# Moving the modulation weight rows: other places in SyncE's load queue, and one block in VectorE's order

## The chip, the cores and the metric

The kernel runs on one core of a Trainium2 chip. The metric is device microseconds of one launch. Three executions of the kernel before took 957.76, 957.87 and 953.32 us, so the median is 957.76 us.

## The reference, cut to what matters

Everything is float32, for one sequence of 256 tokens with 1024 features. A first model (an mLSTM layer, a feed-forward stage, a softmax attention, a second feed-forward stage) is followed by a second model of two layers. Each of these two layers is modulated by a conditioning vector, and the change is about that vector's weights:

```python
c_act = jax.nn.silu(c)                       # 1024 numbers
for l in range(DEPTH):                       # two layers
    mod = c_act @ w_ada[l] + b_ada[l]        # 3072 numbers
    shift, scale, gate = jnp.split(mod, 3, axis=-1)
    h = rmsnorm_2(x, g_pre[l]) * (1.0 + scale[:, None, :]) + shift[:, None, :]
    p = h @ w_in[l]
    ...                                      # convolution branch, attention branch
    x = x + gate[:, None, :] * rmsnorm_2(y, g_post[l])
```

`mod` depends only on `c` and on weights, so it can be computed at any time before layer `l` needs `shift`, `scale` and `gate`.

## The kernel before, in words

**The engines' shares.** TensorE (PE) does all matrix products, VectorE (DVE) and ScalarE (ACT) the elementwise work, GpSimd (POOL) sums of down-projection weights, and SyncE (SP) issues nearly all weight loads from one in-order queue. Every engine has its own fixed program; semaphores join them. Nothing is planned at run time: the order is the order of the code.

**The modulation product.** It is done on DVE. `w_ada` is stored transposed and cut into 48 tiles of 128 x 1024 (512 KB), 24 for each layer; this text calls them ada tiles 0 to 47. `load_ada(first, last)` (L416) issues their loads into `ada_w`, which holds three. For tile n from 3 on it first makes SP wait until DVE has used up tile n - 3. DVE's `ada(count)` (L2165) takes the next `count` tiles in turn: it waits for the tile's load and then multiplies by `c_row`, the silu of `c` broadcast to all partitions, with a sum along the row, one column of `mod`. `modulation(l)` (L2174) adds the bias, `layer_gains(l)` (L2186) forms the gains that layer `l` uses.

**Where DVE takes them.** Tiles 0 to 10 in the 11 steps of the first feed-forward stage, 11 to 14 in its down product, 15 to 20 one for each head in heads 1 to 6 of the first attention (L2453), 21 to 31 and 32 to 35 in the second feed-forward stage, and 36 to 47 in the tail of layer 0: two at L2654, four at L2661 (tiles 38 to 41), then the first half of the convolution branch is gated (`y2_conv`, L2671), two more (42, 43, L2668), the second half is gated, two (44, 45, L2674), and the last two (46, 47, L2708) inside the output norm of token half b = 0, whose end also holds `modulation(1)` and `layer_gains(1)`.

**Where SP loads them.** Among the loads of the ring and of the feed-forward weights. The ring has eight buffers for 64 weight blocks of 1 MB (two of 800 KB). `load(n)` first waits until the product that used the block's last holder is done. Block 51 goes to the buffer of block 43, which holds `w_pw2` of layer 0, so `load(51)` makes SP wait until PE has finished the pointwise product `feat(n + 11, ...)` of layer 0 (L1767 to L1769). `load_up` and `load_down` bring the feed-forward weights into `fring`; `ffn_loads(f)` (L424) holds most of them, with one ada tile for each step.

**PE around the change.** In layer 0 the tail is: pointwise product; wait for `y2_conv` 1; `mix(0, 0, 0, 2)`; wait for `y2_conv` 2; the other mixes; `turn_back(0)` and `turn_back(1)`, which need the norm's diagonals; then layer 1. In the first attention PE's head n needs DVE's scaled probabilities of the head before it, and DVE takes its ada tile after these:

```python
                    if between is not None:
                        between(n)        # ada(1) for n = 1 to 6
```

Of the kernel before, what the change touches and what calls it, by code (L numbers as in the profile page):

```python
# [22 lines left out]
P = 128  # L23
T = 256
TB = T // P
D = 1024
DC = D // P
# [7 lines left out]
DEPTH = 2  # L35
# [76 lines left out]
def model(nc, I, out):  # L112
    with ExitStack() as ctx:
# [5 lines left out]
        def S(name):  # L119

            if name not in sems:
                sems[name] = ctx.enter_context(nc.semaphore(name))
            return sems[name]
# [15 lines left out]
        rstd = sb("rstd", [P, 2 * T])  # L139
# [249 lines left out]
        def _(sp):  # L389
# [26 lines left out]
            def load_ada(first, last):  # L416

                for n in range(first, last):
                    if n >= 3:
                        sp.wait_ge(S("ada_free"), n - 2)  # L420
                    at = D * (n % 24)
                    sp.dma_start(ada_w[:, n % 3, :], I["ada"][n // 24][:, at:at + D]).then_inc(S(f"ada{n % 3}"), 16)

            def ffn_loads(f):  # L424

                a = (0, 21)[f]
                sp.wait_ge(S("up_done"), FF_STEPS * f + 1)
                load_up(f, 2, FF_STEPS * f % 2)
                for i in range(3, FF_STEPS):
                    load_up(f, i, (FF_STEPS * f + i) % 2)  # L430
                    load_down(f, 0, i - 1)
                    load_ada(a + i, a + i + 1)
                load_down(f, 1, 0)
                load_down(f, 1, 1)
                load_down(f, 0, FF_STEPS - 1)
                for i in range(2, FF_STEPS):
                    load_down(f, 1, i)
                    if 3 <= i < 6:
                        load_ada(a + 8 + i, a + 9 + i)
                    if i == 9:  # L440
                        load_ada(a + 14, a + 15)
                load_ada(a + 15, a + 18)

            for m, (k0, k1) in enumerate(FIRST):
# [10 lines left out]
            load_up(0, 0, 0, True)  # L455
            for n in range(8, 16):
                load(n)
            sp.dma_start(c_row[:, :], I["c_2"][0].partition_broadcast(P)).then_inc(S("row_in"), 16)
            load_ada(0, 3)
            product(sp, 11)  # L460
            load_up(0, 1, 1, True)
            for i in (0, 1):
                load_down(0, 0, i, True)
            for n in range(16, 20):
                load(n)
            sp.wait_ge(S("rows_out"), 16)
            row = 3 * P + 1
            sp.dma_start(bass.AP(skewed, 0, [[row, P], [P * row, 8], [1, 3 * P]]),
# [4 lines left out]
                load(n)  # L473
            product(sp, 25)
            sp.wait_ge(S("tok_out"), 20)
            load_ada(18, 21)
            for i in (0, 1):
                load_up(1, i, 1 - i)
                load_down(1, 0, i, True)
            load_ada(21, 24)  # L480
            for n in range(32, 36):
                load(n)
            ffn_loads(1)
# [4 lines left out]
            for l in range(DEPTH):  # L488
                if l > 0:
                    sp.wait_ge(S("vals_done"), 2 * l)  # L490
                sp.dma_start(w_qidx.rearrange("p k n -> p (k n)"), I["w_qidx"][l])\
                    .then_inc(S("small_in"), 16)
                sp.dma_start(w_uv_all, I["w_uv"][l]).then_inc(S("small_in"), 16)
                if l == 0:
                    sp.wait_ge(S("bias_skewed"), 16)
                    for dst, at, wide in ((biasT[:, :, 0:P], 2 * P - 1, P), (biasT[:, :, P:DIAG], P - 1, T)):
                        sp.dma_start(dst, bass.AP(skewed, at, [[3 * P, P], [P * row, 8], [1, wide]]))\
                            .then_inc(S("bias_in"), 16)
                    for n in range(40, 48):
                        load(n)  # L500
                else:
                    for n in range(48, 51):
                        load(n)
                    load_ada(39, 45)
                    load(51)
                    load_ada(45, 48)
                    for n in range(52, 64):
                        load(n)
            sp.wait_ge(S("gains_set"), 2)
# [1291 lines left out]
        def _(dve):  # L1801
# [665 lines left out]
            def layer(l):  # L2467
# [202 lines left out]
                    x = y2[:, 2 * m:2 * m + 2, :]  # L2670
                    v.tensor_tensor(x, x, three(pb[m][:, :], 2), ALU.mult).then_inc(S("y2_conv"), 1)  # L2671

                if l == 0:
                    ada(2)  # L2674

                def gained_out(b, j):

                    dve.wait_ge(S("out_sq"), 4 * l + 2 * b + j + 1)
# [3 lines left out]
                for b in range(TB):  # L2682
# [20 lines left out]
                    else:  # L2703
                        ins.then_inc(S("ms_done"), 1)
                        dve.wait_ge(S("ms_done"), 4 + 2 * l + b)
                        then(v.tensor_scalar(other, half, -0.5, None, ALU.mult))
                        if l == b == 0:
                            ada(2)  # L2708
                        if l == 1:
                            dve.wait_ge(S("row_in"), 32)  # L2710
                            gained_out(b, 0)
# [8 lines left out]
                    dve.wait_ge(S("rstd_done"), nn + 1)  # L2720
                    if l == 0:
                        v.tensor_scalar(diag[:, b, :], ident, y, None, ALU.mult).then_inc(S("diag_done"), 1)
                        if b == 0:
                            modulation(1)
                            layer_gains(1)
                            v.memset(rstd[:, T:T + 1], 1.0)
                            v.tensor_copy(xr[:, :, T:T + 1], mod[:, 1, 0:DC].unsqueeze(2))
                    else:
                        dve.wait_ge(S("gained_out"), 2 * b + 2)
                        dve.wait_ge(S("tokens_cp"), 4)  # L2730
                        for lo, hi in OUT_PARTS[b]:
                            x = h_tok[:, b, lo:hi]
                            v.scalar_tensor_tensor(x, b_ytok[:, b, lo:hi], y, x, ALU.mult, ALU.add)\
                                .then_inc(S("out_ready"), 1)
# [100 lines left out]
```

## Time and profile before

| | |
|---|---|
| median of three runs | 957.76 us |
| the profiled execution's own time | 957.76 us |
| its span | 955.9 us |
| PE busy | 940.4 us (98%) |
| DVE busy | 791.2 us (83%) |
| ACT busy | 278.2 us (29%) |
| POOL busy | 152.0 us (16%) |
| share of PE in the chain that ended last | 88% |
| data moved | 171.8 MB, mean 180 GB/s |

The span is the time from the first to the last instruction; the own time lies 1.86 us above it. Busy time is the time in which an engine had an instruction of its own at work, and PE's matmuls are pipelined, so their durations overlap. The chain that ended last is followed back from the last instruction, at each step to what released it. Times in the rows further down are us from the start of the span, and a bracket at the end of a row says how long the engine stood idle before it and what it was waiting for.

### The profile page before, as it was taken

To read this page: it belongs to the slowest core of one execution; us is meant where nothing else is said; L and a number is where in the kernel's file an instruction comes from. 1 tells how busy PE (TensorE), PEld (TensorE's weight loads), DVE (VectorE), ACT (ScalarE), POOL (GpSimd) and SP (SyncE) were. 2 spreads that over 40 slices of the span, in tenths; PEclk is the share of its full clock that TensorE was granted. 3 is DMA by queue.
4 is the path that set the end of the run, shared out by engine and by line. 5 is a ranking of instruction groups with operands and counts; after the bars stand their busy time and mean duration, and the time that the engine had idled before them with its cause. 6 is when DMAs were issued, how large, how long until landed. Compare 5 with 4: busy or idle time off the path is not lost.

```text
span 955.9 us, 16133 instructions
## 1 busy us (share of the span) xinstructions
PE 940.4 (98%) x6456; PEld 868.9 (91%) x6456; DVE 791.2 (83%) x1690; ACT 278.2 (29%) x622; POOL 152.0 (16%) x139
## 2 busy tenths in 40 slices
PE   9999999999999999999999999999999999999997
PEld 7888999999999998888999999999888878888876
DVE  3778889999999469778799999995699986899963
ACT  1033122221222112254221212221434453624561
POOL 0000210212236520003002131268000000000000
PEclk9999999999999899999999999999999999999999
DMA  8942455363644460558354646446933428442101
GB/s 301 411 184 108 177 190 219 147 261 142 255 156 161 144 268 1 207 213 328 123 198 156 257 146 258 147 164 221 348 133 123 166 88 275 179 136 101 51 1 45
DMA packets 36859, 171.80 MB, mean 180 GB/s; under 512 B 5032, under 2 KB 8880, under 8 KB 23344
## 3 DMA queue, kind: packets, MB, share of 16 engines
q1 hardware_dynamic: 35120, 167.72, 47.7%
q10 hardware_dynamic: 1664, 3.04, 0.9%
q8 instruction: 51, 0.84, 0.4%
q14 instruction: 24, 0.20, 0.1%
HBM read 169.69 MB, written 2.64 MB: 180 GB/s over the span
## 4 chain that ended last, share of the span: by engine, by line
PE 88%; DVE 7%; DMA 2%; issue 1%; ACT 1%; ACTq 0%; SPq 0%; DVEq 0%
PE bank L1376 24%; PE bank L1396 12%; PE bank L1061 9%; PE bank L1479 5%; PE bank L1690 4%; PE bank L1129 3%; PE bank L1594 3%; PE bank L1352 3%; PE bank L1676 3%; PE bank L1575 3%; PE bank L1322 3%; PE bank L1136 3%; DVE work L2245 1%; PE bank L1072 1%; PE bank L1519 1%; DMA ring<-in_ring 1%
## 5 line engine op out<-in xcount | busy, mean ns | idle before, releaser
L1396 PE MATMUL bank<-work,fring 128*128 128x128 f32 x1008 | 118.5, 279 | 3.2 <-DVE work L2264 3.2
L534 POOL TENSOR_TENSOR fring<-fring 128x256 f32<-128x256 f32 x44 | 38.8, 881 | 511.3 <-DMA fring<-in_down 511.3
L1396 PEld LDWEIGHTS bank<-work,fring 128*128 128x128 f32 x1008 | 116.8, 196 | 3.6 <-POOL fring L539 3.2
L2493 DVE SCALAR_TENSOR_TENSOR work<-work,cols 128x256 f32<-128x256 f32 x240 | 98.8, 478 | 1.0 <-ACT work L915 0.5
L1376 PE MATMUL bank<-sq,fring 128*128 128x128 f32 x640 | 84.5, 275 | 0.0
L2170 DVE SCALAR_TENSOR_TENSOR ada_w<-ada_w,c_row 128x1024 f32<-128x1024 f32 x48 | 61.6, 1295 | 27.0 <-DMA ada_w<-in_ada 27.0
L746 ACT ACTIVATE work<-work,cols 128x256 f32<-128x256 f32 x88 | 47.8, 592 | 118.3 <-DVE work L2235 103.7
L2245 DVE SCALAR_TENSOR_TENSOR work<-work,cols 128x256 f32<-128x256 f32 x176 | 78.4, 517 | 2.6 <-ACT work L746 2.6
L1376 PE MATMUL bank<-sq,ring 128*128 128x128 f32 x640 | 78.0, 275 | 0.0
L1376 PE MATMUL bank<-ring,fring 128*128 128x128 f32 x640 | 78.0, 275 | 0.0
L1376 PEld LDWEIGHTS bank<-sq,fring 128*128 128x128 f32 x640 | 77.9, 192 | 0.0
L1376 PEld LDWEIGHTS bank<-ring,fring 128*128 128x128 f32 x640 | 74.8, 192 | 0.1
L1376 PEld LDWEIGHTS bank<-sq,ring 128*128 128x128 f32 x640 | 74.7, 192 | 0.0
L536 POOL TENSOR_TENSOR fring<-fring 128x512 f32<-128x512 f32 x44 | 67.0, 1522 | 3.5
L1690 PE MATMUL bank<-ring,fring 128*128 128x256 f32 x256 | 58.0, 380 | 1.0 <-DVE fring L2671 1.0
L1690 PEld LDWEIGHTS bank<-ring,fring 128*128 128x128 f32 x256 | 48.2, 190 | 8.1 <-DVE fring L2671 1.4
L539 POOL TENSOR_TENSOR fring<-fring 128x256 f32<-128x256 f32 x44 | 46.2, 1050 | 3.4
L1061 PE MATMUL bank<-work,ring 128*128 128x256 f32 x192 | 42.4, 379 | 0.0
L1061 PE MATMUL bank<-xg,ring 128*128 128x256 f32 x192 | 42.3, 380 | 0.0
L1376 PE MATMUL bank<-ring 128*128 128x128 f32 x320 | 42.3, 275 | 0.0
L1061 PEld LDWEIGHTS bank<-xg,ring 128*128 128x128 f32 x192 | 36.3, 190 | 5.1
L1061 PEld LDWEIGHTS bank<-work,ring 128*128 128x128 f32 x192 | 36.3, 190 | 4.9
(416 smaller groups left out, 1771.8 us busy)
## 6 DMA issues: line engine op xcount, KB each, us to landing
ring<-in_ring SPq DMA_DIRECT2D x60, 1024.0 KB, 6.9
fring<-in_up SPq DMA_DIRECT2D x44, 1024.0 KB, 6.9
ada_w<-in_ada SPq DMA_DIRECT2D x48, 512.0 KB, 6.3
fring<-in_down SPq DMA_DIRECT2D x44, 512.0 KB, 4.8
ring<-in_ring SPq DMA_DIRECT2D x2, 800.0 KB, 6.7
bias_skewed<-bias_rows SPq DMA_DIRECT2D x1, 1536.0 KB, 12.7
consts<-in_consts ACTq DMA_DIRECT2D x1, 1128.0 KB, 15.3
ring<-in_ring SPq DMA_DIRECT2D x2, 512.0 KB, 4.8
```

The costliest lines, as they stand in the source:

```text
L534: nc.gpsimd.tensor_tensor(s1, glo, ghi, ALU.add).then_inc(S("down_step"), 1)
L536: nc.gpsimd.tensor_tensor(w[:, 1280:1792], w[:, 0:512], w[:, 256:768], ALU.subtract)\
L539: nc.gpsimd.tensor_tensor(s4, vhi, s2, ALU.subtract).then_inc(S("down_sums"), 1)
L746: nc.scalar.activation(f_t[v][:, c, :], f_u[:, v, c, 0:T], ACT.Identity, bias=col(f"f_conv_b{f}", n), scale=col(f"f_conv_w{f}", n)).then_i ...
L1061: last = mm(bank[:, T * c:T * (c + 1)], w[:, k, at + P * c:at + P * (c + 1)], x[:, k, :], start=(k == 0), stop=(k == nk - 1))
L1376: last = mm(bank[:, P * at:P * (at + 1)], w[:, k, P * c:P * (c + 1)], x[:, k, :], start=(k == 0), stop=(k == 3))
L1396: last = mm(bank[:, at + P * c:at + P * (c + 1)], w[:, P * c:P * (c + 1)], x, start=(i == 0 and at == 0 and c == 0), stop=(i == FF_STEPS - 1),
L1479: last = mm(places[n], x[:, k, :], w[:, k, :], start=(k == 0), stop=(k == 3))
L1690: last = mm(bank[:, 0:T] if apart else bank[:, T * m:T * (m + 1)], y2[:, k, P * b:P * (b + 1)], slot8(load)[:, k, :], start=(k == 4 and (m ...
L2170: v.scalar_tensor_tensor(x, x, 1.0, c_row[:, :], ALU.mult, ALU.mult, accum_out=mod[:, l, j:j + 1])\
L2245: return v.scalar_tensor_tensor(f_t[q][:, c, :], f_u[:, q, c, t:t + T], col(f"f_conv_w{f}", 44 * t + 22 * q + 2 * i + c), f_t[q][:, c, :], ...
L2493: marks[c] = link(v.scalar_tensor_tensor(b_y[:, c, :], b_a[:, c, tap:tap + T], col("conv_w_2", 124 * l + 4 * tap + c), b_y[:, c, :], ALU.m ...
```

## The change

It changes only orders, in five places. In `ffn_loads` ada tile 14 (and tile 35 in the second stage) is loaded after the down tile of i = 6 and no longer after that of i = 9. The loads of `c_row` and of tiles 0 to 2 move from ahead of the wait for product 11 to behind the loads of ring blocks 16 to 19. Tiles 18 to 20 move from ahead of six feed-forward loads to behind them. Ring block 51 is loaded ahead of tiles 39 to 44 and no longer behind them. On DVE, in layer 0, the last two tiles, `modulation(1)`, `layer_gains(1)` and two small writes move out of the output norm's loop to just ahead of it. No tile changes the place in the order of tiles, and no computation is added or dropped.

```diff
--- before.py
+++ after.py
@@ -435,10 +435,8 @@
                 load_down(f, 0, FF_STEPS - 1)
                 for i in range(2, FF_STEPS):
                     load_down(f, 1, i)
-                    if 3 <= i < 6:
+                    if 3 <= i < 7:
                         load_ada(a + 8 + i, a + 9 + i)
-                    if i == 9:
-                        load_ada(a + 14, a + 15)
                 load_ada(a + 15, a + 18)
 
             for m, (k0, k1) in enumerate(FIRST):
@@ -455,14 +453,14 @@
             load_up(0, 0, 0, True)
             for n in range(8, 16):
                 load(n)
-            sp.dma_start(c_row[:, :], I["c_2"][0].partition_broadcast(P)).then_inc(S("row_in"), 16)
-            load_ada(0, 3)
             product(sp, 11)
             load_up(0, 1, 1, True)
             for i in (0, 1):
                 load_down(0, 0, i, True)
             for n in range(16, 20):
                 load(n)
+            sp.dma_start(c_row[:, :], I["c_2"][0].partition_broadcast(P)).then_inc(S("row_in"), 16)
+            load_ada(0, 3)
             sp.wait_ge(S("rows_out"), 16)
             row = 3 * P + 1
             sp.dma_start(bass.AP(skewed, 0, [[row, P], [P * row, 8], [1, 3 * P]]),
@@ -473,11 +471,10 @@
                 load(n)
             product(sp, 25)
             sp.wait_ge(S("tok_out"), 20)
-            load_ada(18, 21)
             for i in (0, 1):
                 load_up(1, i, 1 - i)
                 load_down(1, 0, i, True)
-            load_ada(21, 24)
+            load_ada(18, 24)
             for n in range(32, 36):
                 load(n)
             ffn_loads(1)
@@ -499,11 +496,9 @@
                     for n in range(40, 48):
                         load(n)
                 else:
-                    for n in range(48, 51):
+                    for n in range(48, 52):
                         load(n)
-                    load_ada(39, 45)
-                    load(51)
-                    load_ada(45, 48)
+                    load_ada(39, 48)
                     for n in range(52, 64):
                         load(n)
             sp.wait_ge(S("gains_set"), 2)
@@ -2670,9 +2665,13 @@
                     x = y2[:, 2 * m:2 * m + 2, :]
                     v.tensor_tensor(x, x, three(pb[m][:, :], 2), ALU.mult).then_inc(S("y2_conv"), 1)
 
-                if l == 0:
+                if l + 1 < DEPTH:
                     ada(2)
-
+                    ada(2)
+                    modulation(1)
+                    layer_gains(1)
+                    v.memset(rstd[:, T:T + 1], 1.0)
+                    v.tensor_copy(xr[:, :, T:T + 1], mod[:, l + 1, 0:DC].unsqueeze(2))
                 def gained_out(b, j):
 
                     dve.wait_ge(S("out_sq"), 4 * l + 2 * b + j + 1)
@@ -2704,8 +2703,6 @@
                         ins.then_inc(S("ms_done"), 1)
                         dve.wait_ge(S("ms_done"), 4 + 2 * l + b)
                         then(v.tensor_scalar(other, half, -0.5, None, ALU.mult))
-                        if l == b == 0:
-                            ada(2)
                         if l == 1:
                             dve.wait_ge(S("row_in"), 32)
                             gained_out(b, 0)
@@ -2720,11 +2717,6 @@
                     dve.wait_ge(S("rstd_done"), nn + 1)
                     if l == 0:
                         v.tensor_scalar(diag[:, b, :], ident, y, None, ALU.mult).then_inc(S("diag_done"), 1)
-                        if b == 0:
-                            modulation(1)
-                            layer_gains(1)
-                            v.memset(rstd[:, T:T + 1], 1.0)
-                            v.tensor_copy(xr[:, :, T:T + 1], mod[:, 1, 0:DC].unsqueeze(2))
                     else:
                         dve.wait_ge(S("gained_out"), 2 * b + 2)
                         dve.wait_ge(S("tokens_cp"), 4)
```

## Rows read from the trace of the kernel before

**Rows 1.** Page, part 1: busy us of each engine, share of the span, instructions
```profile
PE 940.4 (98%) x6456; PEld 868.9 (91%) x6456; DVE 791.2 (83%) x1690; ACT 278.2 (29%) x622; POOL 152.0 (16%) x139
```

**Rows 2.** Waits of PE: who was waited for, us in total, times, longest
```profile
PE bank L1396 <- DVE work L2264: 3.2, 2, 3.0
```

**Rows 3.** Timeline, SyncE's queue, layer 0's tail: start, us, instructions
```profile
782.28 12.28 SPq L422 DMA_DIRECT2D ada_w<-in_ada  x6
795.71 0.33 SPq L394 DMA_DIRECT2D ring<-in_ring  x1
796.08 3.74 SPq L422 DMA_DIRECT2D ada_w<-in_ada  x3
```

**Rows 4.** Timeline, PE and DVE, layer 0's tail
```profile
788.61 7.07 PE L1061 MATMUL bank<-work,ring 128*128 128x256 f32 x32
...
792.97 1.22 DVE L2170 SCALAR_TENSOR_TENSOR ada_w<-ada_w,c_row 128x1024 f32<-128x1024 f32 x1 [1.83 <-DMA ada_w<-in_ada]
...
794.12 0.68 DVE L2671 TENSOR_TENSOR fring<-fring,bank 128x512 f32<-128x512 f32 x1
...
795.52 1.89 PE L1690 MATMUL bank<-ring,fring 128*128 128x256 f32 x8
...
798.37 12.35 PE L1690 MATMUL bank<-ring,fring 128*128 128x256 f32 x56 [0.97 <-DVE fring L2671]
...
805.09 0.15 DVE L2686 TENSOR_SCALAR sml<-sml 128x1 f32<-128x1 f32 x1
```

**Rows 5.** DMA view, the issues at 788.88 and at 796.08: KB, us to landing
```profile
ada_w<-in_ada SPq DMA_DIRECT2D x1, 512.0 KB, 4.1
...
ada_w<-in_ada SPq DMA_DIRECT2D x1, 512.0 KB, 7.8
```

**Rows 6.** Timeline, SyncE's queue, the heads of the first attention
```profile
422.52 5.05 SPq L422 DMA_DIRECT2D ada_w<-in_ada  x3
427.62 1.34 SPq L401 DMA_DIRECT2D fring<-in_up  x2
...
432.16 0.51 SPq L422 DMA_DIRECT2D ada_w<-in_ada  x1
```

**Rows 7.** Timeline, DVE, the same heads
```profile
429.36 1.22 DVE L2170 SCALAR_TENSOR_TENSOR ada_w<-ada_w,c_row 128x1024 f32<-128x1024 f32 x1
...
431.51 0.29 DVE L2437 CUSTOM_DVE_ANT_0 sq<-bank,consts 128x128 f32<-128x128 f32 x1 [0.92 <-PE bank L1427]
```

**Rows 8.** DMA view, the issue at 432.16
```profile
ada_w<-in_ada SPq DMA_DIRECT2D x1, 512.0 KB, 14.6
```

**Rows 9.** Busy time, 435 to 440: each engine, granted clock, DMA share, GB/s
```profile
435.00:440.00 5.00, 5.00 (x30) 4.41 (x29) 3.62 (x17) 3.58 (x12) 0.73 (x1) 1.00 1.01 419
```

**Rows 10.** Timeline, start of the first feed-forward stage
```profile
132.87 0.64 SPq L468 DMA_DIRECT2D bias_skewed<-bias_rows  x1
...
146.38 1.29 DVE L2216 TENSOR_TENSOR work<-bank,rstd 128x512 f32<-128x512 f32 x2 [0.40 <-PE bank L1352]
...
156.50 1.22 DVE L1926 TENSOR_TENSOR ring<-fring 128x1024 f32<-128x1024 f32 x1
...
161.71 0.50 PE L1376 MATMUL bank<-ring,fring 128*128 128x128 f32 x3
```

**Rows 11.** DMA view, the issue at 67.06, and the one at 146.74
```profile
c_row<-in_c SPq DMA_DIRECT2D x1, 512.0 KB, 9.9
...
fring<-in_up SPq DMA_DIRECT2D x1, 1024.0 KB, 7.0
```

**Rows 12.** Timeline, second half of the first down product
```profile
320.41 1.22 DVE L2170 SCALAR_TENSOR_TENSOR ada_w<-ada_w,c_row 128x1024 f32<-128x1024 f32 x1
321.23 9.71 SPq L413 DMA_DIRECT2D fring<-in_down  x4
...
327.95 0.72 POOL L534 TENSOR_TENSOR fring<-fring 128x256 f32<-128x256 f32 x1 [0.30 <-DMA fring<-in_down]
```

**Rows 13.** Timeline, PE at the start of the kernel
```profile
1.10 3.78 PE L1095 MATMUL bank<-ones 128*128 128x256 f32 x8 [1.10 <-POOL sml L525]
```

## The prediction

> **What bounds the kernel now.** I read the page's first part, then PE's waits. PE is busy 940.4 of 955.9 us [rows 1]: the kernel is as long as PE's program plus its gaps. The gaps are few: the largest entry in PE's list of waits is 3.2 us in two waits [rows 2]. So an edit can save at most a few us here, and whatever makes PE wait is paid in full. The timelines of SP's queue then say when each moved load can start, the DMA view how long one takes to land, and the timelines of DVE and PE how soon it is needed. SP is in order: a load behind a wait starts after it, whether or not its own buffer is free.
>
> **Step 1, block 51 ahead of tiles 39 to 44.** Before, SP issued tiles 39 to 44 from 782.28 on, block 51 at 795.71, when PE had done the pointwise product, and tiles 45 to 47 from 796.08 [rows 3]. After, tile 39 stands behind block 51 and so behind that wait: it is issued at 796.08. But DVE needs tiles 39, 40 and 41 in `ada(4)` ahead of the first `y2_conv`, and PE needs this for its next mix. There is no deadlock, as the pointwise product needs only what DVE wrote before `ada(4)`. The load issued at 796.08, right behind block 51, took 7.8 us [rows 5]; tile 39 takes its place and lands at 803.9. Each tile is 0.52 MB, and a full queue moved 419 GB/s [rows 9], so one tile lands 1.25 us after another; a tile takes DVE 1.22 us [rows 7]. DVE is through tiles 39 to 41 at 803.9 + 2 x 1.25 + 1.2 = 807.6, `y2_conv` 1 takes 0.68 us [rows 4], and PE starts the mix at 808.3, not 795.52. Tile 42 may be issued when tile 39 is used up, at 805.1, and lands alone 4.1 us later [rows 5], at 809.2; tile 43 follows 1.3 us behind, and DVE ends it at 811.7. `y2_conv` 2 is done at 812.35, and the 56 matmuls behind it start then, not at 798.37 [rows 4]: **+14.0 us**. In formula, they start 8.45 us after tile 39 lands. Lower bound: tile 39 takes 4.1 us like a load on a free queue, +10.3. Upper bound: it lands 1.2 us later, as if one more tile were ahead of it, +15.2. I take 14.0, as the 7.8 us belong to the same instant with the same block ahead.
>
> **Step 2, DVE's block ahead of the output norm.** After step 1 the last four tiles depend on the same chain: each is issued when the tile three before it is used up, lands 4.1 us later and takes 1.2. That gives ends at 813.5, 815.7, 817.0 and 818.8; the five small operations, at the 0.15 us of such an instruction [rows 4], end at 819.6. The norm's first instruction stood at 805.09 [rows 4], 819.1 with step 1. It is 0.5 us late, but PE needs its result only after the mixes, 12.35 us from their start [rows 4], at 824.7: 0. If that cover were gone it would cost the 0.5; if the moved block relieves the end of the norm, it gives back less than PE's gap there of about half a us. I take 0.
>
> **Step 3, tiles 18 to 20 behind six feed-forward loads.** Before, they were issued from 422.52 on, the four up halves (1 MB each) and two down tiles (0.5 MB each) from 427.62, and tile 21 at 432.16 [rows 6]. After, 5.24 MB go ahead of tile 18, which is issued some 4.5 us later, at 427.0. DVE takes tile 18 at 429.36, behind head 4; its next instruction for PE, at 431.51, had a slack of 0.92 us [rows 7]. Two ways to place the landing. By rate: 4.1 us for a single tile hold 1.25 us of data, so 2.85 is fixed; 5.77 MB at 419 GB/s are 13.8; together 422.5 + 16.6 = 439.1. By the same burst: tile 21, behind the same six loads, landed 14.6 us after 432.16 [rows 8], at 446.8, that is 19.2 us after the burst began; a tile was still in the queue ahead, so 1.25 less: 440.5. I take 439.8: DVE stands 10.4 us, PE 10.4 - 0.92 = **+9.5 us**. PE has other work only for its part of one head, which it already does while it waits now. Tiles 19 and 20 are 1.3 us behind each other and DVE wants them 3.4 us apart, so they cost nothing more. Bounds: if the queue were shared so that tile 18 landed early, as on a free queue (4.1 us after 427.0), +0.8; with the full 19.2, +11.4.
>
> **Step 4, `c_row` and tiles 0 to 2 behind blocks 16 to 19.** They are now issued at 132.9, where the bias copy stood [rows 10]. `c_row` behind two ring blocks took 9.9 us [rows 11], so it lands at 142.8; its silu on ACT, a 1024-wide operation like a tile, ends near 144, and DVE's step starts at 146.38 [rows 10]: 0, with 2 us to spare. The 2.1 MB (5.0 us) push the bias copy back, and the up weights issued at 146.74, which landed after 7.0 us [rows 11] at 153.7, meet its end. DVE reads them at 156.50, and PE needs DVE's sums at 161.71 [rows 10], where DVE has about half a us left. The queue was idle for some 2 us before 146.74, so they land 2 to 3 us later: 0 to 1 us. I take 0; bounds 0 and +2.2.
>
> **Step 5, tile 14 (35) three places earlier.** Its wait is for tile 11, which DVE used at 320.41, so it ends at 321.6; SP had just issued the down tile of i = 6, at 321.23, and the next is not due before PE has done its down step, some 3.1 us later [rows 12]. The tile's 1.25 us of transfer lie ahead of that one, for whose data POOL waited 0.30 us [rows 12]; POOL runs ahead of PE, and later down tiles lose the same 1.25 us. 0 for both stages; bounds -0.3 and +1.3 each.
>
> **Step 6, PE after standing still.** PE now stops for about 9.5 and 12.8 us, several times its longest gap in this trace (3.0 us [rows 2]). The only stretch that follows a stop of that kind is the start: eight 256-column matmuls took 3.78 us [rows 13], 472 ns each, while 32 in layer 0's tail took 7.07, 221 ns each [rows 4]. That is the ratio of the clock's two levels, 1.2 and 2.4 GHz, although the column of the granted clock reads full speed. Eight matmuls at the low level lost 2.0 us. I take 2.0 for each of the two stops, **+4.0 us**; bounds 0 and 3.5 each. After the second stop the first eight matmuls are hidden by the wait for `y2_conv` 2, but the 56 behind it are not. The Trainium skill (TensorE: Matmul & The Clock Gate, section on the HAM clock gate) says that half rate is the default and that an idle PE falls back to it; by that rule both stops pay, and by a clock that keeps its level the time would be that of the first rival. The slow start agrees, and no stop in this trace shows the fall.
>
> **Sum.** 955.9 + 14.0 + 9.5 + 4.0 = 983.4 us of span. The profiled execution's own time was 1.86 above its span, so 985.3; it equals the median shown, 957.76.
>
> **Rivals.** (a) The clock keeps its level: 981.3. For it speaks the clock column, against it the start. (b) The queue is shared, and tile 18 lands soon enough for step 3 to cost about 1 and its restart nothing: 985.3 - 8.5 - 2.0 = 974.8. For it: the six loads of the burst overlap; against: tile 21 needed 14.6 us behind them. The Trainium skill (DMA: Bandwidth & Descriptors, section "Queues, rings and completion order") says that each DMA engine consumes a queue's descriptors in ring order; by it the 439.8 of step 3 stands, and by sharing it falls. (c) Step 4 runs out of slack: +1 to 2, 987. (d) Both restarts cost the upper bound: 988. (e) The other side: the ada tiles reach DVE before it stands still, because SP gets past the wait for block 51 while DVE is still in its normalisation. Step 1 turns into a small gain from tiles off the norm and PE's gap of 0.97 before the 56 matmuls [rows 4], and with step 3 hidden as in (b) the time is 957.76 - 0.97 - about 0.5 = 956.3. The point is tile 39's landing at 789.9 or earlier; beyond it each us of lateness costs one. Block 51's wait is for a product that ended at 795.7, after that point, and it is a wait in the code: only if that product ran 10 us earlier could this hold. (f) The edit to the queue does not do what it says, as the tiles were waiting for their own buffers anyway: tile 39 was issued at 782.28, so no.
>
> **Chances.** Forecast 0.50, (a) 0.20, (b) 0.12, (c) and (d) 0.13, (e) and (f) 0.03, something between (b) and none of it 0.02. Low end: (b) with step 1 at 12, 972.8, rounded to 973; high end: the forecast with step 3 at 11.4, step 1 at 15.2 and 3.5 more of clock, 992. A difference of 0.5%, 4.8 us, is about what a measurement of this kernel tells from no change. Every case but (e) and (f) lies above 962.5: slower 0.96, same 0.03, faster 0.01.
>
> **What would show it.** Step 1: SP issues block 51 and then nine tiles, the first at about the end of the pointwise product; DVE waits 12 to 14 us for a load inside `ada(4)`; PE's list of waits has `y2_conv` with over 12 us and a second wait of 2 to 4. Step 2: no wait of PE for the norm over 1 us. Step 3: DVE waits about 10 us for tile 18, PE a little less for the probabilities. Steps 4 and 5: no new PE wait in the feed-forward stages. Step 6: 256-column matmuls of over 400 ns behind a stop. I am wrong if PE's waits grow by less than 15 us, or if most of them lie elsewhere.

## The result and the profile after

The median after is 984.53 us (four executions, 982.79 to 987.02), against 957.37 us in four executions of the kernel before beside them: a ratio of 1.0295, 95% interval 1.026 to 1.0332. The profiled execution's own time is 981.79 us and its span 980.0 us, 24.1 us above the span before. This execution is the fastest of the five of the kernel after on record (spans of 980.0 to 985.2 us): the medians differ by 27.2 us, of which its trace can explain 24.1. Line numbers of the kernel after are 5 lower than before, up to the moved block on DVE.

Page, part 1, of the kernel after: busy us of each engine, share of the span, instructions. PE does 2 us more in 24 us more of span [rows 1], so nearly all the new time is standing still.

```profile
PE 942.4 (96%) x6456; PEld 869.2 (89%) x6456; DVE 788.8 (80%) x1690; ACT 278.3 (28%) x622; POOL 150.5 (15%) x139
```

The chain that ended last, by engine. PE had 88% of it before; now DVE and DMA have 23% together, which is where a learner first sees that the bound is no longer PE alone.

```profile
PE 72%; DVE 17%; DMA 6%; issue 3%; ACT 1%; SPq 0%; ACTq 0%; DVEq 0%
```

Waits of PE in the kernel after: who was waited for, us in total, times, longest. Three entries are new beside [rows 2]: `y2_conv` (step 1), the probabilities of one head (step 3), and the up weights' sums (step 4). They make 11.8 + 10.2 + 1.4 us, where the same three had 1.0 + 0.2 + 0.

```profile
PE bank L1685 <- DVE fring L2666: 11.8, 2, 10.8
PE bank L1433 <- DVE sq L2442: 10.2, 2, 10.0
PE bank L1391 <- DVE work L2259: 3.2, 2, 3.0
PE bank L1371 <- DVE ring L1926: 1.4, 1, 1.4
```

**Layer 0's tail.** SyncE's queue after: block 51 and then nine tiles, as against [rows 3].

```profile
806.92 0.33 SPq L394 DMA_DIRECT2D ring<-in_ring  x1
807.29 16.59 SPq L422 DMA_DIRECT2D ada_w<-in_ada  x9
```

DVE's timeline there (start, us, instruction, idle time before it and what it waited for). Against [rows 4], one wait of 13.27 us for tile 39 stands inside `ada(4)`; tiles 42 and 43 wait 0.46 and 1.20 us.

```profile
813.33 1.23 DVE L2165 SCALAR_TENSOR_TENSOR ada_w<-ada_w,c_row 128x1024 f32<-128x1024 f32 x1 [13.27 <-DMA ada_w<-in_ada]
...
816.98 0.68 DVE L2666 TENSOR_TENSOR fring<-fring,bank 128x512 f32<-128x512 f32 x1
...
818.12 1.23 DVE L2165 SCALAR_TENSOR_TENSOR ada_w<-ada_w,c_row 128x1024 f32<-128x1024 f32 x1 [0.46 <-DMA ada_w<-in_ada]
...
820.55 1.23 DVE L2165 SCALAR_TENSOR_TENSOR ada_w<-ada_w,c_row 128x1024 f32<-128x1024 f32 x1 [1.20 <-DMA ada_w<-in_ada]
```

PE's timeline there. The eight matmuls that took 1.89 us before [rows 4] take 3.77 behind the stop, 472 ns each as at the start of the kernel [rows 13]; the 56 behind them take 12.35, as before. So the lost rate fell wholly into the wait for tile 43.

```profile
817.71 3.77 PE L1685 MATMUL bank<-ring,fring 128*128 128x256 f32 x8 [10.82 <-DVE fring L2666]
822.44 12.35 PE L1685 MATMUL bank<-ring,fring 128*128 128x256 f32 x56 [0.96 <-DVE fring L2666]
...
837.12 2.02 PE L1781 MATMUL bank<-ms,work 128*128 128x128 f32 x16 [0.54 <-DVE ms L2719]
```

Busy time by stretch: PE, PE's weight loads, DVE, ACT, POOL, then the granted clock, DMA share, GB/s. The clock is 0.50, the lower level, from before PE restarts until after it.

```profile
812.00:816.00 4.00, 0.00 (x0) 0.00 (x0) 2.64 (x5) 0.00 (x0) 0.00 (x0) 0.50 0.89 310
816.00:820.00 4.00, 2.29 (x5) 1.83 (x6) 2.89 (x5) 0.00 (x0) 0.00 (x0) 0.50 0.87 292
820.00:824.00 4.00, 3.04 (x11) 2.08 (x10) 3.45 (x6) 0.00 (x0) 0.00 (x0) 0.83 0.85 266
```

**The first attention.** SyncE's queue after: the burst of six loads begins at 422.09, tile 18 is issued at 425.21, 3.1 us later, and DVE has it 14.3 us after that.

```profile
422.09 0.80 SPq L401 DMA_DIRECT2D fring<-in_up  x2
...
425.21 1.94 SPq L422 DMA_DIRECT2D ada_w<-in_ada  x3
```

DVE and PE, the heads of the first attention. DVE waits 10.52 us for tile 18, PE 9.96 for DVE. Its next small matmuls take 0.90 and 1.06 us, against 0.49 and 0.60 one head later. The product of tile 18 itself took 1.91 us, where it took 1.22 before [rows 7]: some 0.7 us of PE's stop.

```profile
439.54 1.91 DVE L2165 SCALAR_TENSOR_TENSOR ada_w<-ada_w,c_row 128x1024 f32<-128x1024 f32 x1 [10.52 <-DMA ada_w<-in_ada]
...
442.73 0.90 PE L1433 MATMUL bank<-consts,sq 128*128 128x128 f32 x3 [9.96 <-DVE sq L2442]
443.43 1.06 PE L1443 MATMUL bank<-nwt,work 128*128 128x256 f32 x2
...
447.66 0.49 PE L1433 MATMUL bank<-consts,sq 128*128 128x128 f32 x3
447.99 0.60 PE L1443 MATMUL bank<-sq,work 128*128 128x256 f32 x2
```

By marks that PE passes in both traces, the 24.1 us come out so (us, after minus before):

| stretch | difference |
|---|---|
| start of the kernel to the first down step | -0.9 |
| from there to the token products: up weights late (step 4) | +1.65 |
| the same stretch: the first down product, 33.13 us in place of 34.34 | -1.2 |
| first attention (step 3) | +11.65 |
| second feed-forward stage (step 5) | +0.1 |
| layer 0's tail (steps 1 and 2) | +12.8 |
| layer 1 | +0.1 |

The -1.2 is not the change. It is a thing that I had overlooked in the trace before: PE stops 3.05 us ahead of the last down products of the first stage (the 3.0 of [rows 2]), and the clock fell there too. The timeline of the kernel before, and its busy time by stretch:

```profile
311.87 34.34 PE L1396 MATMUL bank<-work,fring 128*128 128x128 f32 x280 [3.05 <-DVE work L2264]
```

```profile
311.00:315.00 4.00, 3.13 (x15) 3.16 (x16) 1.38 (x3) 1.67 (x2) 3.77 (x5) 0.50 0.50 200
315.00:319.00 4.00, 4.00 (x25) 4.00 (x25) 3.07 (x7) 0.00 (x0) 1.67 (x2) 0.65 0.03 6
319.00:323.00 4.00, 4.00 (x38) 4.00 (x37) 3.96 (x10) 1.15 (x2) 0.00 (x0) 1.00 0.18 32
```

In the kernel after, the same 280 matmuls behind the same stop took 33.13 us. How long this stop is, and how much half rate follows, changed from one profiled execution to the next; e4, whose program is that of the kernel before up to this point, stopped 4.55 us here.

The -0.9 at the start is not the change either. The same eight matmuls, in the timelines of the kernels before and after, take 3.15 and 2.33 us, because the slow matmuls of the opening [rows 13] gave way to fast ones sooner:

```profile
4.68 3.15 PE L1104 MATMUL bank<-xg,ring 128*128 128x256 f32 x8
```

```profile
4.68 2.33 PE L1099 MATMUL bank<-xg,ring 128*128 128x256 f32 x8
```

In e1 the start cost 3.4 us more than before: PE stopped 2.73 us, as DVE waited longer for a block of the ring (7.93 us, not 5.59), and the clock fell behind that stop too. These two places make up most of what differs outside the places of the change.

### The profile page after: what moved, and what is told of

Its sections match the earlier page's. It is cut to its first block, busy times and chain, and to the rows that moved or that the text cites. A ratio compares the mean times of both kernels' runs of the same rounds, so it can differ in the third digit from the quotient of the medians.

```text
span 980.0 us, 16133 instructions
## 1 busy us (share of the span) xinstructions
PE 942.4 (96%) x6456; PEld 869.2 (89%) x6456; DVE 788.8 (80%) x1690; ACT 278.3 (28%) x622; POOL 150.5 (15%) x139
## 4 chain that ended last, share of the span: by engine, by line
PE 72%; DVE 17%; DMA 6%; issue 3%; ACT 1%; SPq 0%; ACTq 0%; DVEq 0%
PE bank L1371 13%; PE bank L1056 9%; PE bank L1391 9%; PE bank L1474 5%; PE bank L1685 5%; DVE work L2240 4%; PE bank L1124 3%; PE bank L1589 3%; PE bank L1347 3%; PE bank L1671 3%; PE bank L1570 3%; PE bank L1317 3%; DMA ada_w<-in_ada 3%; PE bank L1131 3%; DVE fring L1922 1%
## 5 line engine op out<-in xcount | busy, mean ns | idle before, releaser
L1685 PE MATMUL bank<-ring,fring 128*128 128x256 f32 x256 | 59.9, 389 | 11.8 <-DVE fring L2666 11.8
L1685 PEld LDWEIGHTS bank<-ring,fring 128*128 128x128 f32 x256 | 49.2, 194 | 19.9 <-DVE fring L2666 12.9
## 6 DMA issues: line engine op xcount, KB each, us to landing
bias_skewed<-bias_rows SPq DMA_DIRECT2D x1, 1536.0 KB, 18.8
```

The lines of the kernel that those rows point to most:

```text
L1685: last = mm(bank[:, 0:T] if apart else bank[:, T * m:T * (m + 1)], y2[:, k, P * b:P * (b + 1)], slot8(load)[:, k, :], start=(k == 4 and (m ...
```

## The experiments

Each is one kernel; "median" is set against the kernel before on the same chip, and the segment is the difference of the stretch concerned between the two profiled executions.

### e1: step 1 alone

```diff
-                    for n in range(48, 51):
+                    for n in range(48, 52):
                         load(n)
-                    load_ada(39, 45)
-                    load(51)
-                    load_ada(45, 48)
+                    load_ada(39, 48)
```

> The kernel before with one edit: ring block 51 is loaded ahead of the modulation tiles 39 to 44. Theory (the tiles inherit block 51's wait for the pointwise product, and y2_conv stands behind them on DVE): PE stops about 10.8 us ahead of y2_conv 1 and about 1 us ahead of y2_conv 2, DVE stands about 13 us for tile 39, the span grows by 12.9 us (ratio 1.0135); the granted clock falls in the stop, at no further cost. Rival (the queue's load in that stretch, not the wait, delays the tiles): the tiles are issued from about 782 as before and the span grows by under 4 us.

Measured: 972.59 against 957.94 us, ratio 1.0147 (1.0116 to 1.0179). The tail grew by 14.6 us, where 12.9 was expected. PE's timeline:

```profile
809.03 3.78 PE L1688 MATMUL bank<-ring,fring 128*128 128x256 f32 x8 [10.76 <-DVE fring L2669]
813.96 14.01 PE L1688 MATMUL bank<-ring,fring 128*128 128x256 f32 x56 [1.14 <-DVE fring L2669]
```

The stop is the one of the full change, within 0.06 us, but the 56 matmuls took 14.01 us, not 12.35: here the clock read 0.58 in 814 to 818, in the kernel after it was back sooner. That 1.66 us is nearly all of the difference between 14.6 and 12.8. So step 1 by itself makes the loss in the tail, and what the clock added to it was 1.7 us in one execution and nothing in the other.

### e2: step 3 alone

```diff
-            load_ada(18, 21)
             for i in (0, 1):
                 load_up(1, i, 1 - i)
                 load_down(1, 0, i, True)
-            load_ada(21, 24)
+            load_ada(18, 24)
```

> The kernel before with one edit: tiles 18 to 20 are loaded behind the six feed-forward loads of the first attention. Theory: tile 18 lands 14 to 15 us after its issue, PE stops 10.0 us once, and half clock after the stop adds 1.7 us: span +11.7 us (ratio 1.012). Rival (shared queue): tile 18 lands within 5 us of its issue, span +0 to +2 us. Rival (the stop alone): +10.0 us and no granted clock below 1 behind the stop.

Measured: 967.72 against 957.94 us, ratio 1.010 (1.0068 to 1.0131). The stretch of the heads grew by 11.4 us. DVE's timeline and PE's waits:

```profile
437.85 1.90 DVE L2169 SCALAR_TENSOR_TENSOR ada_w<-ada_w,c_row 128x1024 f32<-128x1024 f32 x1 [9.21 <-DMA ada_w<-in_ada]
```

```profile
PE bank L1437 <- DVE sq L2446: 8.9, 2, 8.6
```

The stop is 1.3 us shorter than in the full change, the half rate behind it longer (0.50 in 440 to 444, 0.71 in 444 to 448): 11.4 less the stop of 8.6 leaves 2.8 us for it. The queue does not share itself out in a way that helps tile 18, so rival (b) is out.

### e3: step 4 alone

```diff
-            sp.dma_start(c_row[:, :], I["c_2"][0].partition_broadcast(P)).then_inc(S("row_in"), 16)
-            load_ada(0, 3)
             product(sp, 11)
...
             for n in range(16, 20):
                 load(n)
+            sp.dma_start(c_row[:, :], I["c_2"][0].partition_broadcast(P)).then_inc(S("row_in"), 16)
+            load_ada(0, 3)
             sp.wait_ge(S("rows_out"), 16)
```

> The kernel before with one edit: c_row and tiles 0 to 2 are loaded behind ring blocks 16 to 19. Theory: 2.1 MB more stand ahead of the up weights of step 2, DVE waits about 1.9 us for them and PE 1.4 us; span +1.6 us (ratio 1.0017, within what can be told), with the wait seen in PE's list as DVE ring. Rival (c_row itself is late): DVE waits for the silu of c_row ahead of its first step and PE stops there. Rival (no effect alone): no new PE wait in the feed-forward stage.

Measured: 959.78 us, ratio 1.0016 (0.9997 to 1.0035), which alone does not tell it from no change. The trace does: DVE waits for the up weights, then PE for DVE, and behind this stop of 2.55 us 16 matmuls take 3.50 us, not 1.95.

```profile
159.17 1.23 DVE L1926 TENSOR_TENSOR ring<-fring 128x1024 f32<-128x1024 f32 x1 [3.03 <-DMA fring<-in_up]
```

```profile
163.97 3.50 PE L1376 MATMUL bank<-ring,fring 128*128 128x128 f32 x16 [2.55 <-DVE ring L1931]
```

DMA view, issues from 125 to 150 (KB each, median us to landing), of the kernel before and then of this one. The up weights took 11.5 us, not 5.9: the bias copy, pushed back, meets them.

```profile
fring<-in_up SPq DMA_DIRECT2D x2, 1024.0 KB, 5.9
bias_skewed<-bias_rows SPq DMA_DIRECT2D x1, 1536.0 KB, 12.7
```

```profile
fring<-in_up SPq DMA_DIRECT2D x2, 1024.0 KB, 11.5
...
bias_skewed<-bias_rows SPq DMA_DIRECT2D x1, 1536.0 KB, 19.6
```

### e6: step 4 with the bias copy moved behind the stage's loads

The edit beside that of e3:

```diff
             load_ada(0, 3)
+            ffn_loads(0)
             sp.wait_ge(S("rows_out"), 16)
             row = 3 * P + 1
             sp.dma_start(bass.AP(skewed, 0, [[row, P], [P * row, 8], [1, 3 * P]]),
                          bass.AP(scratch, 0, [[0, P], [3 * P, 8], [1, 3 * P]])).then_inc(S("bias_skewed"), 16)
-            ffn_loads(0)
```

> The kernel before with c_row and tiles 0 to 2 behind ring blocks 16 to 19, and the bias copy (1.5 MB, DRAM to DRAM) moved from ahead of the first feed-forward loads to behind them. Theory (what costs in that step is the queue's backlog of the copy plus 2.1 MB ahead of the up weights of step 2): with the copy gone from there the up weights land as in the kernel before or sooner, no wait of DVE for them, PE's wait of 1.4 us is gone: 0 against before. Rival (it is c_row or the tiles themselves): the wait stays.

Measured: 957.99 us, ratio 0.9993 (0.9971 to 1.0015); 1.8 us less than e3, but the two intervals overlap, and it is the trace that decides. PE has no wait for the up weights' sums: the 16 matmuls that stopped 2.55 us in e3 follow without a gap, and all issues of up weights in 125 to 160 landed in a median of 6.0 us.

```profile
159.13 3.29 PE L1396 MATMUL bank<-xg,fring 128*128 128x128 f32 x28
162.26 1.95 PE L1376 MATMUL bank<-ring,fring 128*128 128x128 f32 x16
```

So step 4's cost is the meeting of the bias copy, pushed back by 2.1 MB, with the up weights, and not `c_row` being late for DVE.

### e4: step 2 alone

```diff
                 if l == 0:
                     ada(2)
+                    ada(2)
+                    modulation(1)
+                    layer_gains(1)
...
-                        if l == b == 0:
-                            ada(2)
...
-                        if b == 0:
-                            modulation(1)
-                            layer_gains(1)
```

The two small writes move with them.

> The kernel before with one edit: DVE's last two tiles, modulation and gains of layer 1 stand ahead of the output norm. Theory (covered by the mixes): span within 1 us of before, PE's wait for the norm's diagonals stays at about half a us or grows to at most 1.5 us, as the norm of token half 0 ends some 1.5 us later and PE wants it at 810.6. Rival (the block delays the norm in full): PE stops 3 us or more at the first turn_back.

Measured: 957.71 us, ratio 1.0001 (0.9984 to 1.0019); PE's wait for the norm 0.6 us, against 0.5. Nothing, as forecast.

### e5: step 5 alone

```diff
-                    if 3 <= i < 6:
+                    if 3 <= i < 7:
                         load_ada(a + 8 + i, a + 9 + i)
-                    if i == 9:
-                        load_ada(a + 14, a + 15)
```

> The kernel before with one edit: tiles 14 and 35 are loaded three places earlier in the down products. Theory: no new wait of PE in either down product; the 1.2 us that the changed kernel gained in the first one come from the granted clock, which was low for a shorter time behind the 3.05 us stop, and not from this edit: here the stretch of 280 matmuls takes anything from 31.5 to 34.5 us, as the clock falls. Rival (the edit gives the 1.2 us, through POOL's sums or DVE's tile landing sooner): 33.1 us with the same clock as before.

Measured: 958.89 us, ratio 1.002 (1.0001 to 1.0039). In the profiled execution PE's stops ahead of down products are 4.8 us in two (4.6 the longest), against 3.2, and its span is 0.2 us longer than before. The interval just excludes no change; but the same entry read 4.7 us in e4, which has no part of step 5. So the edit costs between 0.1 and 3.7 us in the median, and whether by tile 14 or by chance is open.

### e7: the full change, with spare matmuls in the attention's stop

```diff
                     if between is not None and n > 0:
                         between(n)
+                    if n == 5:
+                        for _ in range(40):
+                            mm(pb[0][:, DIAG:DIAG + P], ones[:, 0:P], ones[:, 0:P], start=True, stop=True)
```

Each call of `mm` makes two matmuls of the trace, here and in e8 and e10.

> The changed kernel with 40 spare matmuls (128 columns, into unused columns of a bank, their result never read) on PE in the first attention, in the stop ahead of head 4's transposes. Theory (the 1.7 us beyond the 10.0 us stop are the clock, which falls as PE stands still): the granted clock stays at 1.00 through and behind the stretch, the matmuls behind it take their full-speed time, and the span is 1.5 us shorter than the changed kernel's (about 978.4 us), if the spare work of some 9 us ends before the probabilities come. Rival (the slow stretch behind the stop is contention with the loads then landing): it stays slow and the span stays at 980 us.

Measured: 987.19 us, ratio 1.030 (1.0267 to 1.0334): no gain in the median, where I expected one. Locally the theory held. Busy time by stretch, to be set against the kernel after, where the clock read 0.50, 0.50 and 0.77 in the first three:

```profile
436.00:440.00 4.00, 4.00 (x38) 4.00 (x38) 0.00 (x0) 0.00 (x0) 0.62 (x1) 1.00 1.02 412
440.00:444.00 4.00, 2.54 (x23) 2.35 (x23) 3.35 (x10) 0.88 (x4) 2.95 (x3) 1.00 0.35 95
444.00:448.00 4.00, 4.00 (x25) 3.59 (x25) 3.15 (x10) 2.21 (x9) 0.00 (x0) 1.00 0.78 245
```

From the probabilities' first matmul to the next but one head's, PE takes 5.06 us (443.81 to 448.87), in the kernel after 6.57 (442.73 to 449.30): 1.5 us is what the low clock cost. As the loads move more here than in the kernel after (245 GB/s, not 168, in 444 to 448), this speaks against the rival, contention with them. Elsewhere this execution was slower: its second feed-forward stage took 4.5 us more than in the kernel after, with a stop of 3.13 us ahead of down products that the other had not, and a clock of 0.73 behind it. Whether the spare matmuls bring this about, or it is the spread named above, stays open, and with it why the median did not fall. The mean granted clock was higher in all four executions (0.989 to 0.991, in the kernel after 0.984 to 0.987), so it was not the clock that took the gain back.

### e8: the kernel before, with six spare matmuls in the 3.05 us stop

```diff
                 down(1, 0)
                 down(1, 1)
+                if f == 0:
+                    for _ in range(6):
+                        mm(pb[0][:, T:2 * T], ones[:, 0:P], ones[:, :], start=True, stop=True)
                 down(0, FF_STEPS - 1)
```

These matmuls begin their bank's sum anew, so a part of the first stage's down product is left out of the output; the amount of work is otherwise that of the kernel before.

> The kernel before with 6 spare matmuls (256 columns, 2.65 us in all, result never read) on PE in the 3.05 us stop of the first down product. Theory: that stop is long enough for the granted clock to fall to 0.50, which costs 2.8 us behind it; filled, the clock stays at 1.00 and the 280 matmuls behind it take 31.5 us, not 34.3: span -2.8 us (ratio 0.997). Rival (the 2.8 us are late down sums from POOL, not the clock): no change. Rival (the clock's fall depends on the moment of the stop): the fall may still come for the 0.4 us left, or not.

Measured: 956.06 against 957.81 us, ratio 0.9989 (0.9972 to 1.0006). PE's timeline:

```profile
307.97 2.76 PE L1411 MATMUL bank<-ones 128*128 128x256 f32 x12
310.72 31.50 PE L1396 MATMUL bank<-work,fring 128*128 128x128 f32 x280
```

The clock reads 1.00 in every 4 us from 303 to 319, and the 280 matmuls take 31.50 us, not 34.34: the stop of 3.05 us had cost 2.84 us of low clock beside itself. In the median 1.75 us of it show, and the interval includes no change. The executions beside it bear on this: of the 29 of the kernel before, six have a mean granted clock of 0.999 or more, as high as in e8's trace, which has no fall, and their spans are 951.5 to 954.7 us; the other 23 have a median span of 956.5. With the stop filled, the clock was 0.998 or more in all twelve executions. By these clocks not every execution of the kernel before pays for a fall, though only one of them has a trace.

### e9: step 1, with DVE's tiles moved behind both `y2_conv`

SyncE's edit is that of e1; DVE's:

```diff
-                if l == 0:
-                    ada(4)
                 dve.wait_ge(S("conv_gate"), l + 1)
...
                     else:
-                        if l == 0:
-                            ada(2)
                         product(dve, n + 11)
...
                 if l == 0:
-                    ada(2)
+                    ada(8)
```

> Step 1 of the change alone (block 51 ahead of tiles 39 to 44), but with VectorE's products of tiles 38 to 43 all moved behind both y2_conv operations, where the last two stood already (eight products in a row there). This tells apart whether the loss comes from the tiles' late landing as such or from where VectorE waits for them. Theory (the place decides): the convolution's output no longer waits for tile 39, so TensorE's stop at the y2_conv semaphore (10.8 us in the run with step 1 alone) and the half clock behind it are gone; the eight products, four of which wait for their landing, now stand between y2_conv and VectorE's share of the output norm, and come out there as a new stop of TensorE: the tiles land near 802 us, the last product ends near 805 to 807, where the norm was ready for VectorE near 797 to 798, so some 8 us, and up to 1.5 more if the clock falls: 8 to 10 over the kernel before, 966 to 968, ratio 1.008 to 1.010. Rival (the landing alone decides, the place doesn't matter): as with step 1 alone, about 972, ratio 1.014.

Measured: 967.48 against 957.85 us, ratio 1.010 (1.0076 to 1.0123). PE's timeline: no stop at `y2_conv`, all 64 mixes in one run, and one stop at the norm.

```profile
794.76 13.98 PE L1688 MATMUL bank<-ring,fring 128*128 128x256 f32 x64
818.92 5.90 PE L1784 MATMUL bank<-ms,work 128*128 128x128 f32 x32 [10.19 <-DVE ms L2716]
```

The norm's products start 24.16 us after the first mix, in the kernel before 15.05 (795.52 to 810.57): 9.1 us late. They take 5.90 us, not 3.97 and a gap of 0.54, so 1.4 more. Both sizes are near what was expected, but the way there was longer than I wrote: the eighth product ended at 812.6, not at 805 to 807, and the last two inside the norm (the tile of each is loaded only when the one three before it is used up) at 817.7. The place where DVE waits decides how much of a late landing is paid; it can't be hidden wholly here, since ten tiles, each behind the use of an earlier one, need 22 us from 795.6.

### e10: the kernel before, with two other edits

```diff
                 down(1, 1)
+                if f == 0:
+                    for _ in range(6):
+                        mm(pb[0][:, T:2 * T], pc("mask_st", P, P), ones[:, :], start=False, stop=False,
+                           skip_group_check=True)
...
                     else:
-                        if l == 0:
-                            ada(2)
                         product(dve, n + 11)
...
                 if l == 0:
-                    ada(2)
+                    ada(4)
```

> The kernel before with two edits of another kind, and none of the change: six spare matmuls (zero weights, added to a sum that is open, so the result stays) in TensorE's 3.05 us stop ahead of the last down product of the first FF group in the first feed-forward stage, and VectorE's products of tiles 40 and 41 moved from between the two y2_conv operations to behind both. Theory: the spare matmuls keep the granted clock at 1.00, so the 280 matmuls of that stretch take about 31.5 us and not 34.3 (-2.8 in the profiled run; the stop itself varies from run to run, so -1 to -3 in the median), and TensorE's wait of 0.97 us at the second y2_conv goes (-1.0): -2 to -4 us in all, ratio 0.996 to 0.998. Rival: matmuls with zero weights don't hold the clock, or the products come out at the output norm instead: within 1 us of before, ratio 0.999 to 1.001.

(The tiles that move are 42 and 43, in the counting of this text.)

Measured: 954.88 against 957.85 us, ratio 0.997 (0.9955 to 0.9985), twelve executions of it. The spare matmuls add zero to an open sum. In the profiled execution the stop is down to 0.54 us, the clock is 1.00 over the span, and the 64 mixes run in one piece:

```profile
310.65 31.50 PE L1396 MATMUL bank<-work,fring 128*128 128x128 f32 x280 [0.54 <-DVE work L2268]
...
792.07 13.98 PE L1694 MATMUL bank<-ring,fring 128*128 128x256 f32 x64
805.89 1.95 PE L1790 MATMUL bank<-ms,work 128*128 128x128 f32 x16
```

It is the fastest kernel of this study, by 3 us or 0.3%. Which share of that each edit has in the median wasn't separated; in the traces they are 2.8 us and 1.2 us.

## Why the prediction was right, step by step

The forecast of 985.3 us is 0.8 above the median and 3.5 above the profiled execution. The mechanism was right: the two big waits, where they lie and what they cost within some 2 us. That the sum came so near the median is partly luck. Taken one at a time, steps 1 to 5 cost 14.65, -0.2, 9.8, 1.8 and 1.1 us in the medians, 27.1 together, and the whole change 27.2; the forecast had 16.0, 0, 11.5, 0 and 0 with the clock counted in, 27.5. So it was about 3 us too high for steps 1 and 3 and about 3 too low for the rest, each of these within an interval of some 2 to 3 us either way.

In the profiled execution, the span of 983.4 us misses the measured 980.0 by 3.4: step 1 and its clock were 3.15 too large, step 3 and its clock 0.15 too small, step 4 1.65 too small, and start and first down product came out 2.1 lower by chance.

**Step 1** (14.0 us, and 2.0 for the clock): 12.85 in the full change, 14.6 in e1. Of the 3.15 too much, 2.0 are the clock, which the wait for tile 43 hid here, and 1.8 the landing of tile 39, taken as 7.8 us after the issue and measured at 6.0. The formula, mixes restart for good 8.45 us after tile 39 lands, gave 8.45 + 813.3 = 821.8, and the trace shows 822.44, 0.7 later: tile 43 came 2.4 us behind tile 42, not 1.3. The like row was the right one to look for, but that 7.8 belonged to a queue that still held earlier tiles [rows 3, 5]; here it was empty but for block 51. Low bound 10.3, high bound 15.2: inside.

**Step 2** (0): 0. PE's wait at the norm is 0.54 us in [rows 4]'s kernel and in the kernel after, and e4 shows the edit alone at 1.0001.

**Step 3** (9.5, and 2.0 for the clock): the stop is 9.96 us, the low clock 1.7. Tile 18 landed 17.4 us after the burst's first issue, between the 16.6 and 18.0 of my two ways of placing it; that the burst takes SyncE 3.1 us and not 4.5 did not matter, as both count from its start. The product of tile 18, 0.7 us longer than before, was in no term. In e2 the sum is 11.4.

**Step 4** (0): 1.65 in the full change, and a stop of 2.55 us with the clock behind it in e3. This is the term that was wrong in kind. I let the up weights land at the end of the bias copy and gave back "some 2 us" of idle queue; they took 9.6 and 11.7 us in the kernel after, not 7.0 [rows 11], and DVE had no slack left. Rival (c) named this outcome. e6 shows the culprit: without the copy beside them, they cost nothing.

**Step 5** (0, bounds -0.3 and +1.3): no new wait in the kernel after; e5's 1.0001 to 1.0039 leaves up to 3.7 us open, so whether this term was right isn't shown.

**Step 6** (2.0 each): the fall is real at both stops, so rival (a) is out, though of the 4.0 us only 1.7 were paid in the profiled execution, whose 981.79 us lie nearer to that rival's 981.3 than to the forecast. e7 and e2 put the price at 1.5 and 2.8 us behind the attention's stop, and the full change and e1 at 0 and 1.7 behind the tail's, where I had missed that the first eight slow matmuls hide in the wait for tile 43 and the rest may be back at full rate by then. The sentence that no stop in the trace before shows the fall was false: [rows 2]'s 3.0 us stop does, with 0.50 in the granted clock and 2.8 us of cost. Whoever takes the windows around every stop over 2 us sees it. By the Trainium skill (TensorE: Matmul & The Clock Gate, section on the HAM clock gate) a PE that idles falls to half rate; the traces agree, with 472 ns for a 256-column matmul behind the stop and 221 ns in the undisturbed run.

## What to carry to other kernels

In an in-order load queue, a load starts no earlier than the last wait ahead of it ends: before one is moved past a wait, compare the time at which that wait ends with the time at which the first consumer stands ready. Where PE is busy 98% of the span, each new stop is paid in full and then once more in low clock, so price a stop of 2.5 us or more at 0 to 2.8 us above its length, the range of the stops here, and look for stops that the kernel already has: filling one with spare matmuls gained most of the edits tried, 2.8 us in the trace. If a consumer must wait, put it behind the work that other engines are waiting for, which in e9 saved 5 of 15 us.

## What the runs showed of the hardware

- The clock fell behind stops of 2.55 us (e3), 2.73 (e1) and every one from 2.96 to 10.8 in the twelve traces. It did not behind those of 1.38 us (the kernel after, where 16 matmuls then took 2.05 us, against 1.95 without a stop), 1.8 (e3, e6, e8) and 2.1 (e7, e9), nor behind one of 2.67 us at the start of e6, so length alone did not decide between 2.5 and 2.7. With stops of the same length (10.76 and 10.82 us), it was back earlier in one execution than in the other, and 56 matmuls took 12.35 and 14.01 us.
- The kernel before spreads over 10 us of span in 29 executions (951.5 to 961.3), and the shorter ones tend to have the higher mean granted clock (1.000 in the shortest, 0.993 in the longest).
- Spare matmuls with all-zero weights were followed by a clock of 1.00 as those of ones were (e10, e8).
- At the start of the kernel matmuls take 472 ns [rows 13], the time of the lower level, while the column of the granted clock reads 1.00 there: the column did not show the low level there, while it did behind the stops above. The change to fast matmuls came at another time in each execution (eight matmuls from 4.68 us on took 3.15 us before and 2.33 after).
- The product of a tile took 1.91 us, not 1.22, when POOL was at work beside it (tile 18, after, and 1.90 in e2). POOL's own 128x256 addition that began beside it took 1.58 us, where the shortest of that line take 0.72. The Trainium skill (GPSIMD Engine Reference, section 1, Specifications) says that POOL shares its SBUF interfaces with VectorE, in contention when a DVE instruction has two SBUF inputs. The rows agree, the tile's product being such an instruction; no run here separates it.
- A 1.5 MB copy of the bias rows took 12.7 us to land in the kernel before and 18.8 to 19.6 with 2.1 MB of other loads ahead of it; the up weights issued behind it took 10.7 to 11.5 us instead of 5.9.
